# Retention with zero-padded operands and a divided rotation, with three smaller edits, in a two-block transformer kernel

## The reference, cut to what matters

```python
def retention(q, k, v):                      # 4 heads, dk = 64, dv = 128, chunks of C = 128
    q = rotary(q); k = rotary(k) * dk ** -0.5
    scores = einsum('bhnid,bhnjd->bhnij', qc, kc) * decay
    o_intra = einsum('bhnij,bhnje->bhnie', scores, vc)
    chunk_kv = einsum('bhnjd,hj,bhnje->nbhde', kc, k_decay, vc)
    def step(state, kv): return state * g_chunk + kv, state
    o_inter = einsum('bhnid,hi,nbhde->bhnie', qc, q_decay, r_prev)
    return o_intra + o_inter

def rotary(x):
    return concatenate([x1 * cos - x2 * sin, x1 * sin + x2 * cos], -1)

def hgrn2(q, f_logit, i, lb):                # 4 heads of 128
    log_f = log_sigmoid(f_logit)             # lb is 0 here
    k = sigmoid(-f_logit)
    b = cumsum(log_f)                        # within a chunk
    attn[t, s] = sum_k q[t, k] * exp(b[t, k] - b[s, k]) * k[s, k]     # s <= t
```

## Time and profile before

| | us |
|---|---|
| timed runs, median of 3 | 2588.99 (2585.32 to 2596.64) |
| the profiled execution itself | 2613.81 |
| its span | 2612.0 |
| retention, first load to last copy | 1617.15 to 1700.2 |
| gated recurrence, first load to last product | 2327.18 to 2484 |

### The profile page before, as it was taken

The page is one execution under the profiler, slowest core; times in us unless marked ns, Lnnn a source line. Parts: engine busy times, 40 slices in busy tenths (PEclk is TensorE's granted clock), DMA queues, the critical chain, the costliest instruction groups (busy, mean ns, idle before and its releaser), DMA issues. The chain is left out here.

```text
span 2612.0 us, 34392 instructions
## 1 busy us (share of the span) xinstructions
PE 2218.1 (85%) x12244; PEld 1825.9 (70%) x12244; DVE 1290.0 (49%) x2211; ACT 1029.8 (39%) x1828; POOL 584.1 (22%) x672
## 2 busy tenths in 40 slices
PE   7996997999797599999289997968859799956768
PEld 5885887999685466675278885758748687845657
DVE  3333665555543666665451210357755343417843
ACT  3333654555431255554231210046543233327632
POOL 1003101522010122231110001446522000027822
PEclk9997998999898699999699998579989899987879
DMA  4787776321344399995652312243163424141152
GB/s 152 215 239 198 221 219 165 98 64 40 118 146 171 126 359 370 355 342 209 217 206 97 113 49 77 61 87 73 37 219 108 153 95 148 69 135 47 42 184 90
DMA packets 216721, 399.15 MB, mean 153 GB/s; under 512 B 90513, under 2 KB 111377, under 8 KB 203905
## 3 DMA queue, kind: packets, MB, share of 16 engines
q1 hardware_dynamic: 177008, 314.52, 38.0%
q10 hardware_dynamic: 28384, 61.62, 6.2%
q0 software_dynamic: 11184, 21.13, 2.2%
HBM read 300.16 MB, written 114.85 MB: 159 GB/s over the span
## 5 line engine op out<-in xcount | busy, mean ns | idle before, releaser
L78 PE MATMUL pe_acc<-pe_w,hT 128*128 128x512 f32 x960 | 222.3, 393 | 0.0
L78 PEld LDWEIGHTS pe_acc<-pe_w,hT 128*128 128x128 f32 x960 | 181.7, 190 | 37.8
L78 PE MATMUL ex_gu<-hT,ex_xT 128*128 128x512 f32 x792 | 194.2, 401 | 0.8 <-DVE hT L2349 0.8
L2349 DVE TENSOR_TENSOR hT<-ex_raw,hT 128x2048 fp32r<-128x2048 f32 x66 | 150.9, 2288 | 87.1 <-ACT hT L2320 87.1
L78 PE MATMUL pg_acc<-hT,pg_w 128*128 128x512 f32 x768 | 180.0, 396 | 8.9 <-DVE pg_w L257 8.9
L78 PEld LDWEIGHTS pg_acc<-hT,pg_w 128*128 128x128 f32 x768 | 145.5, 190 | 42.4 <-DVE pg_w L257 9.3
L78 PEld LDWEIGHTS ex_gu<-hT,ex_xT 128*128 128x128 f32 x792 | 147.4, 189 | 34.5 <-DVE hT L2349 1.2
L2320 ACT ACTIVATE hT<-ex_raw 128x2048 fp32r<-128x2048 f32 x66 | 126.2, 1913 | 41.4 <-PEq L47 23.9
L296 DVE COPY pe_o<-pe_acc 128x512 f32<-128x512 f32 x28 | 19.3, 690 | 206.7 <-PE pe_acc L78 206.7
L1725 PE MATMUL ab_op<-ab_v,ab_pT 128*128 128x64 f32 x1024 | 121.3, 272 | 0.0
L2278 PE MATMUL ex_dn<-ex_wd,ex_hT 128*128 128x512 f32 x264 | 118.7, 592 | 0.8 <-ACT ex_hT L2314 0.8
(11 more groups left out here) (473 smaller groups left out, 4990.9 us busy)
## 6 DMA issues: line engine op xcount, KB each, us to landing
ex_raw<-in_w_gate SPq DMA_DIRECT2D x33, 1024.0 KB, 7.2
ex_raw<-in_w_up SPq DMA_DIRECT2D x33, 1024.0 KB, 11.1
ex_wd<-in_w_down SPq DMA_DIRECT2D x33, 1024.0 KB, 14.2
pe_raw<-in_even_w_in SPq DMA_DIRECT2D x6, 2048.0 KB, 9.1
pg_raw<-in_odd_w_in SPq DMA_DIRECT2D x5, 2048.0 KB, 9.4
scr_q<-pa_o SPq DMA_DIRECT2D x32, 256.0 KB, 3.8
scr_k<-pa_o SPq DMA_DIRECT2D x32, 256.0 KB, 3.8
hT<-scr_k SPq DMA_DIRECT2D x16, 512.0 KB, 6.8
```

What stands on the lines that cost most here:

```text
L78: mm = pe.matmul(out, a(p, k), b(q, k), start=(k == 0 and i == 0), stop=(k == n - 1 and i == 2))
L2349: dve.tensor_tensor(split(s, LO)[:, :, g, :], raw[:, s % NW, g, :].rearrange("p (k n) -> p k n", k=8), split(s, HI)[:, :, g, :].bitcast(F3 ...
```

## The change

1. **Zero padding in retention.** The transposed k goes into `kz`, one 128-row operand per head, whose other 64 rows stay zero; `state` has one 128-row block per head, whose other half stays zero. Scores and q by state are then products of 128 rows. The two clears are done once by DVE. The state update is four instructions on 64 partitions instead of two on 128.
2. **Divided rotation.** POOL makes the even half (two products, a difference), DVE the odd half (two products, a sum, `turn_odd`, two tiles ahead). The copies out of PSUM (four instead of two) go from DVE to ACT (`turn_back`). x of tile 0 is loaded first, and the rotation waits for its table alone.
3. **First tile order.** In `project` with a front, tile 1 is turned by PE behind the sixth of the eight k steps of tile 0's product. With lx = 1, ACT's and DVE's turn of tile 0 come one step earlier, right behind the weight split. In `Rows.load` the gain row comes behind the first tile's loads (also in the output stages).
4. **Pairs.** The further blocks' loop goes 7 rounds with two bodies under one condition.
5. **Single level differences.** DVE makes one difference b - mid of 512 columns per level; ACT takes two exponentials of 256 columns, with scale -1 and +1. In unit 0, DVE makes k's products (`keys_first`) and POOL only q's.

```diff
@@ project
+                def first_steps(k):
+                    pe.wait_ge(lo_ok, k + 1)
+                    if r and k == nk - 2:
+                        r.pe_turn(pe, 1)
...
-                            for t in range(j + 1 if j else 0, min(j + 2, NT)):
+                            for t in range(j + 1 if j else 0, min(j + 2, NT) if j else 1):
                                 r.pe_turn(pe, t)
...
-                        at_step(s, (r.act_turn, lx + 2, act), (r.act_x, lx, act), (r.act_y, 0, act))
+                        if s > lx + 2:
+                            at_step(s, (r.act_turn, lx + 2, act))
+                        elif lx and s == 2:
+                            r.act_turn(act, 0)
+                        at_step(s, (r.act_x, lx, act), (r.act_y, 0, act))
...
                             split_lo(dve, 0)
-                        at_step(s, (r.dve_turn, lx + 2, dve), (r.dve_x, lx, dve), (r.dve_y, 0, dve))
+                            r.dve_turn(dve, 0)
+                        if s > lx + 2:
+                            at_step(s, (r.dve_turn, lx + 2, dve))
+                        at_step(s, (r.dve_x, lx, dve), (r.dve_y, 0, dve))
@@ experts, further
-            with eng.Fori(1, NOV) as j:
-                with eng.If(n > j):
-                    body(j)
+            with eng.Fori(0, (NOV - 1) // 2) as r:
+                with eng.If(n > r * 2 + 1):
+                    for i in range(2):
+                        body(r * 2 + (i + 1))
@@ retention, SP
-                sp.dma_start(cs[:, :, :], C["ret_cs"].rearrange("(t p) n -> p t n", p=P)).then_inc(consts_in, 16)
+                sp.dma_start(x[:, 0, :], rows_in[0:P, 0:1024]).then_inc(x_in[0], 16)
+                sp.dma_start(cs[:, :, :], C["ret_cs"].rearrange("(t p) n -> p t n", p=P)).then_inc(cs_in, 16)
@@ retention, POOL (0, t1, t2) and DVE (32, t3, t4)
+                eng.tensor_tensor(a[:, u, :, :], first[0], first[1], ALU.mult).then_inc(products, 1)
+                eng.tensor_tensor(b[:, u, :, :], second[0], second[1], ALU.mult).then_inc(products, 1)
+                eng.wait_ge(products, 2 * (t + 1))
+                eng.tensor_tensor(rot[:, t % 4, :, c0:c0 + 32], a[:, u, :, :], b[:, u, :, :], op).then_inc(step, 1)
@@ retention, PE
-                            mm = pe.matmul(o, qkT[p0:p0 + 64, u, 4 + j, :], state[p0:p0 + 64, u, j, :], start=False, stop=True)
+                            mm = pe.matmul(o, qkT[:, u, 2 + j, :], state[:, u, h, :], start=False, stop=True)
...
-                            mm = pe.matmul(sps[h % 2][:, j * P:(j + 1) * P], qkT[p0:p0 + 64, u, 2 + j, :], qkT[p0:p0 + 64, u, j, :],
-                                           start=True, stop=True)
+                            mm = pe.matmul(sps[h % 2][:, j * P:(j + 1) * P], kz[:, u, h, :], qkT[:, u, j, :], start=True, stop=True)
@@ retention, DVE
                         if s + 1 < NT:
                             decay(s + 1)
+                        if s + 2 < NT:
+                            turn_odd(s + 2)
...
-                        for j in range(2):
-                            dve.scalar_tensor_tensor(out=state[:, 1 - u, j, :], in0=state[:, u, j, :], scalar=gch[:, j:j + 1],
-                                                     in1=kv[:, j * RDV:(j + 1) * RDV], op0=ALU.mult, op1=ALU.add).then_inc(state_ok, 1)
+                        for h in range(RH):
+                            r, j = slice(64 * (h % 2), 64 * (h % 2) + 64), h // 2
+                            dve.scalar_tensor_tensor(out=state[r, 1 - u, h, :], in0=state[r, u, h, :], scalar=gch[r, j:j + 1],
+                                                     in1=kv[r, j * RDV:(j + 1) * RDV], op0=ALU.mult, op1=ALU.add).then_inc(state_ok, 1)
@@ retention, ACT
+                    act.activation(qkT[:, u, 0:2, :].rearrange("p j n -> p (j n)"), tp[0][:, 0:2 * P], ACT.Copy).then_inc(T_ok, 1)
+                    for b in range(2):
+                        r = slice(64 * b, 64 * b + 64)
+                        act.activation(kz[r, u, :, :].rearrange("p (j b) n -> p j b n", b=2)[:, :, b, :],
+                                       tp[0][r, 2 * P:4 * P].rearrange("p (j n) -> p j n", j=2), ACT.Copy).then_inc(T_ok, 1)
+                    act.activation(qkT[:, u, 2:4, :].rearrange("p j n -> p (j n)"), tp[1][:, 0:2 * P], ACT.Copy).then_inc(T_ok, 1)
...
                 for t in range(NT):
+                    if t + 1 < NT:
+                        turn_back(t + 1)
                     act.wait_ge(o_ok, t + 1)
@@ hgrn2
-                        act.activation(ex[:, g % 2, :], df[:, g % 2, :], ACT.Exp).then_inc(ex_ok, 1)
+                        for half, sign in enumerate((-1.0, 1.0)):
+                            act.activation(ev[:, :, half, :], dv[:, :, half, :], ACT.Exp, scale=sign).then_inc(ex_ok, 1)
...
+                            if n == 0 and half == 0:
+                                continue
...
-                        dve.tensor_tensor(dv[:, :, 0, :], mid, bv[:, :, 0, :], ALU.subtract).then_inc(df_ok, 1)
-                        dve.tensor_tensor(dv[:, :, 1, :], bv[:, :, 1, :], mid, ALU.subtract).then_inc(df_ok, 1)
+                        dve.tensor_tensor(whole(df[:, g % 2, :], m), whole(b[:, :], m), mid, ALU.subtract).then_inc(df_ok, 1)
+                        if n == 0 and l:
+                            keys_first(l - 1)
+                    if n == 0 and part == 3:
+                        keys_first(NL - 1)
```

More of the change, by code:

```diff
@@ L222, in _ @@
                             pe.wait_ge(copied[u], uses[g][j])
-                        before = (lambda k: pe.wait_ge(lo_ok, k + 1)) if g == 0 and j == 0 else None
+                        before = first_steps if g == 0 and j == 0 else None
                         if ch["kind"] == "row":
@@ L321, in _ @@
                             split_hi(act, 0)
+                            if not lx:
+                                r.act_turn(act, 0)
                         if s >= lx + 4:
@@ L520, in load @@
                 sp.dma_start(self.e[c][:, u, :], rows(self.expert_rows[0], c * NT + t)).then_inc(self.tile_in[u], 16)
+        if t == 0 and self.post is not None:
+            sp.dma_start(self.prow[:, :], self.post.partition_broadcast(P)).then_inc(self.post_in, 16)
     def pool_begin(self, pool):
@@ L2449, in _ @@
                 sp.dma_start(gch[:, :], C["ret_gchunk"]).then_inc(consts_in, 16)
-                for t in range(NT):
+                for t in range(1, NT):
                     if t >= 4:
@@ L2453, in _, with rotate @@
                         sp.wait_ge(o_ok, t - 3)
-                        sp.wait_ge(m1, 4 * (t - 3))
+                        sp.wait_ge(m1, 2 * (t - 3))
+                        sp.wait_ge(m2, 2 * (t - 3))
                     sp.dma_start(x[:, t % 4, :], rows_in[t * P:(t + 1) * P, 0:1024]).then_inc(x_in[t % 4], 16)
+            def rotate(eng, t, products, step, op, c0, a, b):
+                u = t % 2
+                eng.wait_ge(x_in[t % 4], 16 * (t // 4 + 1))
+                if t >= 4:
+                    eng.wait_ge(turned, t - 3)
+                    eng.wait_ge(decayed, t - 3)
+                xv = x[:, t % 4, 0:512].rearrange("p (h d) -> p h d", d=64)
+                c = cs[:, t, 0:32].unsqueeze(1).to_broadcast([P, QK, 32])
+                s = cs[:, t, 32:64].unsqueeze(1).to_broadcast([P, QK, 32])
+                even, odd = xv[:, :, 0:32], xv[:, :, 32:64]
+                first, second = ((even, c), (odd, s)) if c0 == 0 else ((even, s), (odd, c))
+                eng.tensor_tensor(a[:, u, :, :], first[0], first[1], ALU.mult).then_inc(products, 1)
+                eng.tensor_tensor(b[:, u, :, :], second[0], second[1], ALU.mult).then_inc(products, 1)
+                eng.wait_ge(products, 2 * (t + 1))
+                eng.tensor_tensor(rot[:, t % 4, :, c0:c0 + 32], a[:, u, :, :], b[:, u, :, :], op).then_inc(step, 1)
@@ L2476, in _ @@
+                    rotate(pool, t, m1, rotated, ALU.subtract, 0, t1, t2)
             @block.tensor
@@ L2861, in split, with whole, pool_products @@
             return x.rearrange("p (n h m) -> p n h m", h=2, m=m)
+        def whole(x, m):
+            return x.rearrange("p (n m) -> p n m", m=2 * m)
+        def pool_products(g):
+            return g if g <= NL else 2 * g - NL
         def of_unit(buf, n):
@@ L3113, in _ @@
                         if G % UC == 0:
-                            pe.wait_ge(qk_ok, 2 * NL * (n + 1))
+                            pe.wait_ge(qk_ok, pool_products(NL * (n + 1)))
+                            if n == 0:
+                                pe.wait_ge(first_ok, NL)
                             pe.wait_ge(kb_ok, n + 1)
```

93 lines of the change are left out of this document (48 added, 45 removed).

## The result

| | before | after |
|---|---|---|
| timed runs, median of 5 | 2592.36 us | 2575.43 us (2573.27 to 2576.84) |
| profiled execution | 2613.81 us | 2576.84 us |

The ratio is 0.9937, with an interval of 0.9919 to 0.9955: the change saves 16.9 us, 0.65%. Forecast were 36.5 us and a range that ended at 2575.0. The direction was right, the size was not.

The account below looks back on a forecast made before the run. Each stage was taken to have its own limit, retention PE at the low clock. Terms -34.8 - 3.8 + 1.4 + 0.2 - 4.0 - 1.0 gave -42.0; with 5.5 given back, 2589.0 - 36.5 = 2552 us, range 2535 to 2575.

Parts of the forecast that it names:

- I give back a quarter of this, 5.5: Retention: timed runs may have had an early clock rise worth 22 us; 5.5 us was taken off the gain.
- rival 2: Retention's clock yields nothing, 17%: it stays at 1.2 GHz (2574), or second form, timed runs had it high already (-20, 2569).
- The clock in the changed kernel: Retention: TensorE's clock near 1.0 from the second step on, with uniform full-height work and no mode changes.
- Start of retention, -5.4: Retention's start: x first and rotation divided between POOL and DVE bring the first transpose 5.4 us earlier.
- DVE's tile, 3.9 us, and steps of 4.2 to 4.65: Retention's loop: DVE needs 3.9 us a tile; four steps take 4.65 us each and two 4.2.
- rival 3: Retention: DVE and POOL rotating together disturb each other, 2.2 us a step, 13 us less gain, 2565; 12%.
- Load ring "comes last": Retention: x's load, DVE's odd rotation, state and score product make 9.3 us in two steps, 4.65 each, tiles 4 to 7.
- Further loop, -3.8: Further blocks' loop on POOL: seven of 14 rounds go, 4.1 us, less the longer condition's cost: -3.8 us.
- First projection, +1.4: First projection: second product starts at 28.5 instead of 27.11, +1.4 us (0 to 1.9).
- Joined front, +0.2: Joined front: +1.2 us on the deciding chain, 1.0 given back by moving the gain row: +0.2 (-0.6 to +1.2).
- Recurrence, -5.0: Gated recurrence: start -4.0 us from seven of POOL's 14 products moved to DVE, loop -1.0 from single differences.

Follow-up runs that it names:

- no_pad: Changed kernel with retention's padding undone (scores and q by state with 64 contracting rows again), divided rotation kept; 2588.3 us, ratio 0.9974.
- pool_rot: Changed kernel with the rotation's division undone, POOL making both halves of every tile; 2576.18 us, ratio 0.9939.
- after_again: The changed kernel unchanged, run again; 2574.99 us, ratio to before 0.9944.
- ret_only: Kernel before with the changed kernel's retention alone (padding and divided rotation); 2581.87 us, ratio 0.9953.
- best_ring: Changed kernel without first tile order, DVE rotating only tiles 0 and 1's odd halves, x in eight buffers loaded at start; 2576.2 us, ratio 0.9925.
- start_div: Changed kernel with DVE making the odd half of tiles 0 and 1 only, POOL both halves of tiles 2 to 7; 2577.35 us, ratio 0.9938.

## Why the prediction was wrong

**The step that failed** is the last one: "I give back a quarter of this, 5.5". The text had the right cause for the 24.8 us between the profiled execution and the timed runs, and even its size: a step of 5.5 us at the high clock (5.17 measured) and 22 us in all (23.6 between the two executions of before). It then gave back only a quarter, for which it names no row, though all three timed runs lay 17 us and more below the profiled one. In seven looks before's retention has a median of 63.0 us, so of the 83.0 that the sum started from 20.0 were to be given back, not 5.5. Giving back all 22 makes 2569, the second form of rival 2. The measured gain lies there, 3.1 us short of that rival's 20. That it comes so near is partly luck: from trace to trace retention gained 28.0 us instead of 34.8, and the recurrence about 1 instead of 5.0, and something else made up a part of this.

The rule of the Trainium skill (TensorE: Matmul & The Clock Gate, Part 1) that sustained activity releases the array was on that rival's side. Six of the seven looks at before's retention have the clock up 8 to 25 us after PE's first transpose, as the rule would have it; the seventh, the trace that was shown, has PE full for over 60 us at 0.50, and no_pad for 53, against it. The prediction was right that the trace contradicts the rule and wrong to take one trace for the kernel.

Of the rest, point by point:

- **The clock in the changed kernel: right.** High from the third step on, but for 3.4 us, and a rise at 15 to 17 us in eight looks with padding. The reason given, "mode changes gone" and "full-height work", is at most half right: the four looks at reordered half-height products rise after 15 to 26 us too, without full height, though four looks are few.
- **Start of retention, -5.4: -4.3.** First transpose 7.49 us after the first load instead of 11.83; with the division undone (pool_rot) it is 9.39, so x first and the wait for the table alone bring 2.4 us and the division 1.9. The rotation starts 4.7 us after the first load, when its table has landed, not 4.2. DVE and POOL begin the rotation together and both slow down: the row of 1624.89 waits for POOL, whose products now take 0.9 and more instead of 0.69.
- **DVE's tile, 3.9 us, and steps of 4.2 to 4.65: too short.** Outputs come 5.2 us apart on average (36.1 us in seven steps), for rotation operations take 0.8 to 0.95 beside POOL's, not 0.4, and the state updates 0.37, not 0.3. That is rival 3's mechanism, acting inside the forecast: against the old step at the high clock (5.17) the loop gained nothing. What retention gained beside its start is that its clock no longer rises late. In the looks it goes from a median of 63.0 us (seven) to 54.4 (after, after_again, ret_only): -8.6, or -10.6 by the means; ret_only gave 10 to 12.
- **Load ring "comes last": the mechanism is in the trace, its price is open.** In the changed kernel DVE waits 1.94 and 1.96 us for x with its odd rotation, the state stands behind that rotation, and PE then waits 2.17 and 2.19 us for the state (0.85 a third time). That is the path as forecast, with steps of 8.2 and 6.6 us between ones of 4.1 where 4.65 was said. The 0.8 us of best_ring were measured where DVE has no rotation in the loop and do not price it here. Taking DVE's rotation out of the loop (start_div) brought 4.2 us on the average of the two looks, ring and slowed operations together.
- **Further loop, -3.8: -4.0.** From the last scatter to the next stage's first load it is 19.5 us in all nine looks without pairs and 15.5 in all eleven with them.
- **First projection, +1.4: +1.45** at the second product. At the end of the projection the seven looks with the new order are 0.6 later than the thirteen without, within a spread of 4 us.
- **Joined front, +0.2: -0.3**, from its first load to the end of its projection (354.4 against 354.7 in the mean, looks with one order 3 to 4 us apart, so nothing that can be told).
- **Recurrence, -5.0: -1.2 by the median of nine looks, -0.8 by their mean.** The start brought 2.0, not 4.0, because a product on DVE takes 0.42 to 1.09 beside POOL's (forecast 0.34) and a level 1.14 (2307.93 to 2314.78 in six), not 0.95. The loop gave 0.8 back instead of bringing 1.0: the doubled exponential costs 0.09 a level, not 0.04.

The ledger by the traces is -8.6 to -10.6 for retention, -4.0, -0.8 to -1.2, +0.6 and -0.3, together -13.1 to -15.5. The measured -16.9 lies 1.4 to 3.8 beyond it. Stick-breaking, whose code is the same everywhere, took 171.0 us on average in the seven looks behind before's retention and 168.1 in after, after_again and ret_only. That is 2.9 us, enough for what is missing; whether it follows from what retention did or is chance is not settled.

## What to carry to other kernels

When a profiled execution lies well off its timed runs, find the stretch that makes the difference before pricing anything in it: here it was 20 us in the very stage that was to be changed, and half of the apparent gain with it. For small float32 matmuls as here, do not alternate shapes with different contracting rows; run equal ones together, one open sum per bank. Splitting work over DVE and POOL at the same time pays only where the critical path waits for it, and even there the division won 1.9 us of the rotation's 4.3. Price a buffer or a load ring in the kernel that has the consumer in question: taken away elsewhere it shows next to nothing.

## What the runs showed of the hardware that was not expected

- **The clock's rise is a draw.** Identical code in retention saw it after 20 to 74 us. Stick-breaking took 168.0 to 172.9 us from its first output product to its last, with the clock rising 14 to 21 us after its first matmul: 168.0 to 168.3 in nine looks, all with the rise at 14 to 15, and 169.6 to 172.9 in eleven with the rise at 19 to 21. Latent attention with its output stage varied from 601 to 611. Each of these scatters is larger than any edit outside retention.
- **Alternation costs 0.2 us and more a pair.** Two instructions of one shape, between two of the other, take 0.42 us at the high clock; among their like they take 0.22 (128 rows) or 0.14 (64 rows, 0.55 for eight); at the low clock 0.73 against 0.43 in the changed kernel (1644.73 to 1645.16).
- **DVE and POOL slow each other.** DVE's 128x256 product takes 0.42 us alone and 0.95 beside POOL's, POOL's 0.72 alone and 0.90 to 1.19 beside DVE's:

```profile
L2490 DVE TENSOR_TENSOR re_t<-re_x,re_cs x8: 410/942/952, 1622.5 to 1658.1; 128x256 f32<-128x256 f32 x8
L2490 POOL TENSOR_TENSOR re_t<-re_x,re_cs x8: 897/902/1186, 1623.1 to 1656.7; 128x256 f32<-128x256 f32 x8
```
